# The last MoE batch written out, with dummy products on TensorE ahead of the last expert's down units and its scatter

## The reference, cut to what matters

```python
def expert_choice_moe(h, w_router, w1, w3, w2):      # N_EXPERTS = 16, EXPERT_FF = 1024
    cap = EC_CAPACITY * S // N_EXPERTS               # 32 tokens for each expert
    aff = jax.nn.softmax(jnp.einsum('bsd,de->bse', h, w_router), axis=-1)
    vals, idx = lax.top_k(aff.transpose(0, 2, 1), cap)
    xg = h[bidx, idx]
    h1 = jnp.einsum('becd,edf->becf', xg, w1)
    h3 = jnp.einsum('becd,edf->becf', xg, w3)
    out = jnp.einsum('becf,efd->becd', jax.nn.silu(h1) * h3, w2) * vals[..., None]
    return jnp.zeros_like(h).at[bidx, idx].add(out)
...
x = x + expert_choice_moe(rmsnorm_2(x, norm_moe[i]), ...)
ple_gate = jax.nn.sigmoid(rmsnorm_2(x, norm_ple[i]) @ ple_gate_w[i])
x = x + ple_gate * (p[i] @ ple_w[i])
```

## Time and profile before

| | us |
|---|---|
| median of 3 runs | 1885.49 |
| lowest, highest | 1884.97, 1887.38 |
| span of the profiled execution, first to last instruction | 1886.9 |
| TensorE busy | 1546.9 (82%) |
| chain that ended last, waits for `moe_w` transfers | 37% |

### The profile page before, as it was taken

How to read it: one execution, slowest core, us unless ns; L and a number is a source line. 1 busy time by engine, 2 the same in 40 slices (tenths; PEclk the granted TensorE clock), 3 DMA queues, 4 the chain that set the end, 5 groups by cost and what they waited for, 6 DMA issues and landing times.

```text
span 1886.9 us, 29888 instructions
## 1 busy us (share of the span) xinstructions
PE 1546.9 (82%) x12670; PEld 1134.2 (60%) x12670; DVE 633.5 (34%) x934; ACT 517.6 (27%) x921; POOL 193.9 (10%) x215
## 2 busy tenths in 40 slices
PE   9999999999999999656665666999998665666657
PEld 8999899998798885232322324997873322223225
DVE  3556653677656452000000003655540000000005
ACT  3434344556444532000000003454521000000003
POOL 1042000011141100000000002310100000000003
PEclk9999999999999999898888878999999888988888
DMA  9364679423554479999999999644499999999994
GB/s 305 122 211 164 210 234 290 135 90 113 182 166 140 136 318 380 424 426 425 424 428 426 427 425 348 197 146 149 174 381 405 423 427 423 429 425 426 427 424 144
DMA packets 166895, 563.67 MB, mean 299 GB/s; under 512 B 10559, under 2 KB 120027, under 8 KB 133896
## 3 DMA queue, kind: packets, MB, share of 16 engines
q1 hardware_dynamic: 161092, 553.88, 76.0%
q10 hardware_dynamic: 5700, 8.31, 1.3%
HBM read 561.08 MB, written 5.23 MB: 300 GB/s over the span
## 4 chain that ended last, share of the span: by engine, by line
PE 51%; DMA 37%; DVE 4%; issue 3%; ACT 3%; POOL 1%; ACTq 0%; DVEq 0%; POOLq 0%; SPq 0%
DMA ring<-in_moe_w 37%; PE bank L1003 20%; PE bank L1271 7%; PE bank L1685 4%; PE bank L955 3%; PE bank L1334 2%; PE bank L1708 2%; PE bank L1118 1%; ACT ring_r L1758 1%; PE bank L1110 1%; PE bank L1148 1%; PE bank L1543 1%; ACT big L1806 1%; PE bank L1343 1%; PE bank L1083 1%
## 5 line engine op out<-in xcount | busy, mean ns | idle before, releaser
L1685 PE MATMUL bank<-ring,big 128*32 128x256 f32 x3840 | 281.6, 443 | 196.2 <-DMA ring<-in_moe_w 193.8
L1003 PE MATMUL bank<-big_r,ring_r 128*128 128x256 f32 (+1 forms) x2856 | 355.4, 284 | 0.0
L1685 PEld LDWEIGHTS bank<-ring,big 128*32 128x32 f32 x3840 | 146.4, 123 | 337.9 <-issue 296.7
L1003 PEld LDWEIGHTS bank<-big_r,ring_r 128*128 128x128 f32 (+1 forms) x2856 | 346.2, 191 | 3.0 <-issue 2.2
L2156 DVE TENSOR_TENSOR ring_r<-ring,ring_r 128x2048 fp32r<-128x2048 f32 (+2 forms) x113 | 260.1, 2307 | 135.9 <-ACT ring_r L1758 134.6
L1806 ACT ACTIVATE big<-bank 128x512 f32<-128x512 f32 (+2 forms) x186 | 87.9, 491 | 561.8 <-PE bank L955 355.6
L1758 ACT ACTIVATE ring_r<-ring 128x2048 fp32r<-128x2048 f32 (+2 forms) x117 | 219.3, 1884 | 13.2 <-issue 7.3
L1708 PE MATMUL bank<-ring,big 128*32 128x512 f32 x1024 | 137.5, 634 | 74.8 <-DMA ring<-in_moe_w 57.7
L2551 DVE SCALAR_TENSOR_TENSOR big<-big,bank 128x256 f32<-128x256 f32 x32 | 13.5, 421 | 460.1 <-ACT big L2059 460.1
L1271 PE MATMUL bank<-ring_r,big_r 128*128 128x512 f32 x576 | 136.6, 396 | 0.7 <-DVE big_r L2163 0.7
L1271 PEld LDWEIGHTS bank<-ring_r,big_r 128*128 128x128 f32 x576 | 107.9, 189 | 25.5 <-DVE ring_r L2156 1.1
(11 more groups left out here) (213 smaller groups left out, 1474.5 us busy)
## 6 DMA issues: line engine op xcount, KB each, us to landing
ring<-in_moe_w SPq DMA_DIRECT2D x120, 2048.0 KB, 23.7
ring<-in_moe_w SPq DMA_DIRECT2D x128, 1024.0 KB, 24.9
ring<-in_w_in SPq DMA_DIRECT2D x28, 1024.0 KB, 5.4
ring<-in_od_w_in SPq DMA_DIRECT2D x22, 1024.0 KB, 6.0
ring<-in_ev_w_in SPq DMA_DIRECT2D x20, 1024.0 KB, 5.5
big<-in_moe_w SPq DMA_DIRECT2D x8, 2048.0 KB, 11.0
ring<-in_ev_w_out SPq DMA_DIRECT2D x8, 1024.0 KB, 5.0
ring<-in_od_cmp_w SPq DMA_DIRECT2D x8, 1024.0 KB, 8.3
```

Of the source, the lines that this page charges most:

```text
L1003: ins = unit[0].mark(mm(dst, lhsT, rhs, start=start and n == 0, stop=stop and n == len(terms) - 1))
L1685: ins = mm(banks[5 + up][32 * j:32 * j + 32, 0:256], xg[:, k, q, :], wv[:, r, 256 * j:256 * (j + 1)], start=k == 0, stop=k == KC - 1)
```

## The change

The last batch is taken out of the hardware loop, which now makes two trips, and is written out behind it. Conditions that asked whether a batch is written out now ask for batch 0. In the last expert of the last batch (`closing`), TensorE runs three dummy products ahead of each of the four down units, before it waits for the unit, and one dummy product between the last down unit and the wait for `ob_ready` ahead of the scatter. A dummy multiplies the identity (128x128) with 256 columns of constants into columns 256 to 511 of bank 6, which nothing reads. That makes 13 dummies for each of the two layers. Nothing else differs, on no other engine.

```diff
+                def keep_warm(n):
+
+                    for _ in range(n):
+                        mm(banks[6][:, T:2 * T], ident, big[:, con_at:con_at + T], start=True, stop=True)
+
...
-                                spare = isinstance(b, int) and q < 2 and part == 1
+                                spare = isinstance(b, int) and b == 0 and q < 2 and part == 1
...
-                        if isinstance(b, int) and q == 0:
+                        if isinstance(b, int) and b == q == 0:
                             keep_after(3)
...
                         pe.wait_ge(hT_ready, m + 1)
+                        closing = isinstance(b, int) and b > 0 and q == BATCH - 1
                         for j in range(4):
+                            if closing:
+                                keep_warm(3)
                             U = Unit()
...
                         ins.then_inc(down_done, 1)
+                        if closing:
+                            keep_warm(1)
                         pe.wait_ge(ob_ready, m + 1)
...
                 batch(0)
-                with pe.Fori(0, NE // BATCH - 1) as b:
+                with pe.Fori(0, NE // BATCH - 2) as b:
                     w.enter(b, BATCH * MOE_UNITS)
                     batch(b + 1)
-                    w.leave(NE // BATCH - 1)
+                    w.leave(NE // BATCH - 2)
+                batch(NE // BATCH - 1)
```

## The result

The change takes 1893.0 us in the median of 5 runs (1891.88 to 1894.64) against 1885.49 (1884.97 to 1887.38) before: a ratio of 1.0039, 95% interval 1.0029 to 1.0050. Run again beside 27 runs of the kernel before, it gave 1893.87 against 1886.16, ratio 1.0038 (1.0024 to 1.0051). So it is 7 to 8 us slower. I had forecast 0.6.

What follows compares the result with a forecast made beforehand. In the MoE stages TensorE waits for weights from a full DMA. Dummies delay the fourth down unit more than the held clock gains: 14.10 against 13.79 and 13.78, 0.3 a layer, 0.6 in sum, 1886.1 us; range 1884.0 to 1888.8.

Steps and rivals of the forecast that it cites:

- my 0.3: Forecast delay of DVE's split, line 2115, in each layer: 14.10 against 13.79 and 13.78 us after the first down unit's start.
- Call it zero: Last expert: times counted from the first down unit's start, 1153.00 and 1838.97; everything up to it hides under `moe_w` transfers.
- The base, line 2115 at 13.79 and 13.78: Before the change, DVE's split was taken to start 13.79 and 13.78 us after the first down unit, first and second layer.
- 1.4 under that span: The runs' median, 1885.49, stands 1.4 us under the profiled span, 1886.9; the same 0.6 was added to both.
- 0.1 for each change: Each change of form between dummies and down units costs 0.1 us; seven ahead of the fourth unit, 0.7.
- my 8.44: Fourth down unit's start after the first group began: dummies 5.16, three down units 2.58, seven changes of form 0.7.
- my 3.85: From the scatter's start, forecast at 10.25, to DVE's split at 14.10, at full clock with four DVE copies.
- 14.10: Forecast start of DVE's split, line 2115, after the change, in us from the start of the last expert's dummies.
- the way back: Change from full-width products to column groups, read between the gather and the first up unit as 0.08 us.
- rival (b): Each change of form drains the array, 0.36 us each: 2.1 later a layer, 4.3 in sum, 1889.8 us; chance 0.04.
- which continuous products should hold: From the fourth down unit on, full clock: unit 1.06, scatter 1.99; gains 0.88 and 1.6, only partly reaching the chain.
- Rival (c): Clock falls despite the dummies, before the last group, or had fallen when they begin: 3.4 later a layer, 1892.3 us; chance 0.03.

Runs made afterwards that it cites:

- before_again: The kernel before, unchanged, run again for a second profile: 1886.53 us, ratio 0.9998.
- written_out_only: The change with no dummies at all, only the last batch written out: 1889.3 us, ratio 1.0010 against the kernel before.
- gaps_only: The change with three dummies ahead of only the third and fourth down units, one ahead of the scatter: 1886.67 us, ratio 0.9998 against the kernel before.
- first_two_groups: The change with three dummies ahead of only the first and second down units, one ahead of the scatter: 1885.49 us, ratio 0.9996 against the kernel before.
- in_the_loop: Kernel before, batch not written out; each looped batch's last expert gets three dummies before down units three and four, one before the scatter: 1885.68 us, ratio 0.9996.
- in_the_loop_and_behind: in_the_loop plus one dummy between scatter and tile 0's transposes and two before the first gate products: 1885.22 us, ratio 1.0003 against the kernel before.
- two_each: The change with two dummies instead of three ahead of each down unit, one ahead of the scatter: 1888.62 us, ratio 1.0013 against the kernel before.
- three_without_last: The change without dummies ahead of the fourth down unit, three ahead of the others, one ahead of the scatter: 1888.86 us, ratio 1.0017 against the kernel before.
- change_and_up_parts: The change plus three dummies ahead of each of the last expert's four up parts: 1891.44 us, ratio 1.0034 against the kernel before.
- change_again: The change, unmodified, run again for a second profile: 1893.87 us, ratio 1.0038 against the kernel before.
- change_and_behind: The change plus one dummy between scatter and tile 0's transposes and two before the first gate products: 1893.32 us, ratio 1.0037 against the kernel before.
- six_dummies: The change with six dummies instead of three ahead of each down unit, one ahead of the scatter: 1902.97 us, ratio 1.0088 against the kernel before.

## Why the prediction was wrong

**The direction and the mechanism were right.** Four groups make TensorE late at the fourth unit, the wait on the DMA goes, and the clock holds. The place is shown by the number of dummies: level with before with two groups (either two), +2.9 with two dummies each, +3.1 with three groups, +7.7 with all, +16.0 with twice as many (medians, each against the kernel before of its own set). The size was off by more than ten times: the sum began in the wrong place, and it stood on an unusual execution. The account, from the start of the fourth up part to DVE's split (timelines, us, first and second layer):

| kernel | fourth up part takes | to line 2115 or its like |
|---|---|---|
| before | 1.93, 1.93 | 17.58, 17.57 |
| before_again | 1.93, 1.93 | 16.62, 16.54 |
| written_out_only | 1.93, 1.93 | 17.64, 16.69 |
| gaps_only | 3.30, 1.93 | 16.50, 15.46 |
| first_two_groups | 3.51, 3.35 | 16.57, 16.35 |
| in_the_loop | 3.33, 3.64 | 16.51, 18.97 |
| in_the_loop_and_behind | 1.93, 1.93 | 15.56, 15.42 |
| two_each | 1.93, 1.93 | 16.47, 16.47 |
| three_without_last | 1.93, 1.93 | 16.57, 16.57 |
| change_and_up_parts | 1.93, 1.93 | 18.19, 18.19 |
| change | 1.93, 3.64 | 18.20, 20.16 |
| change_again | 1.93, 3.64 | 18.20, 21.99 |
| change_and_behind | 2.78, 3.64 | 20.85, 21.99 |
| six_dummies | 3.39, 3.41 | 25.01, 24.85 |

The kernel before has 17.1 in the mean of its two profiles; change, change_again and change_and_behind have 20.2: 3.1 a layer, 6.3 in all, of 7.7 measured. Of the 2.8 a layer above my 0.3, the slow parts make 2.0 (20.2 against 18.20), the base 0.5, the changes of form 0.35.

**1. "Call it zero": the first down unit's start.** This step failed, and by the table it is the largest part. I took the start of the first down unit as the same before and after, because all ahead of it "hides under `moe_w` transfers". It does not come at a fixed time after the landing: the fourth up part takes 1.93, or up to 3.64 when it meets the low clock. The kernel before hides this. Its own trace shows it, one expert ahead of the last in the first layer:

```profile
1119.71 3.64 PE L1685 MATMUL bank<-ring,big 128*32 128x256 f32 x32 [1.28 <-DMA ring<-in_moe_w]
...
1125.47 2.78 PE L1708 MATMUL bank<-ring,big 128*32 128x512 f32 x24 [0.52 <-issue]
...
1149.21 1.93 PE L1685 MATMUL bank<-ring,big 128*32 128x256 f32 x32 [1.46 <-DMA ring<-in_moe_w]
```

The fourth unit still waits 1.28 for its transfer, and the scatter starts at 1131.35, 11.64 after the part; in the last expert, with a part of 1.93 at 1149.21, it is 12.67. The two profiles of the kernel before have 28 experts each whose fourth part and down units wait for transfers. In 33 of these 56 the fourth part is slow (2.77 to 3.64). In 28 of the 33 the scatter starts 11.64 to 11.67 after the part's start and takes 1.99. In the 23 with a part of 1.93 it starts 11.61 to 12.67 after it, and takes 3.29 to 3.68 in all but one. So before the change a slow part mostly costs nothing, and even leaves the clock up for the scatter.

With the wait on the DMA gone, so is the cover: the delay goes through in full, and where the first dummies meet the low clock as well, more than in full (18.20 to 21.99). I had counted what the dummies cost, but not what the removed wait had absorbed. Four of the six ends of change, change_again and change_and_behind have a slow part. It does not need all four groups: in_the_loop's second layer, with two, comes at 18.97. In time it is shown less well: 1.9 us between change_and_behind and change_and_up_parts, with overlapping intervals.

**2. The base, line 2115 at 13.79 and 13.78.** The rows were right, but of an execution with the low clock in the last down unit of both layers. before_again has 12.82 and 12.74: by it the base was 1.0 too late in each layer. A run's time lies 1.8 over its span (1886.53 for 1884.7, 1893.78 for 1892.0), so the profiled execution of before was a run of about 1888.7, above all that I had timed. I had read the median "1.4 under that span" as an offset, when it said that the profiled execution took longer than the timed ones. And both profiles may flatter the change: their four ends all have a fast fourth part and then a slow scatter. For an end with a slow part, 11.65 to the scatter and 3.68 from a full-clock scatter to the split (as in every end with one here) would make 15.3, an estimate. No profile caught such an end of the kernel before.

**3. "0.1 for each change".** The fourth unit starts at 8.96 against my 8.44. A dummy is 0.43 as predicted (3.78 - 2.49 = 1.29 for three more), so the seven changes cost 8.96 - 5.16 - 2.58 = 1.22, 0.17 each, within my bounds of 0 and 0.36. The fourth unit is 0.52 later than forecast; from the scatter to line 2126 it then takes 3.68 for my 3.85, so 0.35 is left there (14.45 for 14.10). The sum behind the 0.1 was loose as well: it names 0.118 a record and computes with 0.115, and with 0.118 the way back would have cost nothing. The Trainium skill's rule, "TensorEngine Tiling (Array Packing)", Key Properties, that changing the mode drains the array, bears more than I gave it; rival (b) in its full size, 0.36, did not come.

**4. The clock "which continuous products should hold".** It held through the scatter. Rival (c) named 1892.3, close to what was measured, but for another reason: a fall ahead of the last group, which no profile has. Its other condition, a clock that "had fallen when they begin", did come, in the second layers of change_again and change_and_behind: the first group takes 2.93 for 1.56 there. In the change's first profile the clock then fell 5 us after the scatter began, behind the stretch with 1.09 busy of 2.80, on the first gate products: 1.43 in each layer, and in neither of the second profile, though the same stretch has 1.09 busy there too. In the kernel before's two profiles the low clock lay on the scatter and had risen again by line 1334. So part of what the dummies buy at one place may be paid at the next. A slow line 1334 does reach the end of the program: from the second layer's split (line 2115 or its like) to the end of the span it is 35.56 to 35.60 in the three profiles that have one there (change, three_without_last, change_and_up_parts), and 34.10 to 34.44 in the other eleven. That filling the stretch keeps line 1334 at full clock fits two profiles, but is not shown: the profiles beside them had the full clock without it.

**5. The forecast that the batch written out is worth nothing** stands within some 2 us: 1.0010 in the kernel that has nothing else, 0.9998 and 0.9996 in two that have dummies too. The instruction queue carried 0.19 MB more (1.47 for 1.28), where I had estimated 0.12 for both layers. Whether its 12 packets cost anything stays open.

What also stays open: the rest of about 1.4 us between 6.3 and 7.7, and why two_each and three_without_last are 2.9 and 3.1 slower than before, though their profiles (16.47, 16.57) are level with before_again. Two terms could fill it, and neither is shown to: the gate products (2.9 in one of three profiles, 1 in the mean), and ends of the kernel before with a slow part. If these are as frequent as in its other experts, 33 of 56, its mean end is 16.1 and not 17.1, by the estimate of 15.3. A few profiles can't give a distribution.

No version tried is measurably faster than the kernel before.

## What to carry to other kernels

Filler in a wait is free only as long as the sum of filler and work stays under the arrival of the last transfer, and it also uses up the slack that absorbs a late start, even where it stands only ahead of units that really wait. Check the sum against the last landing with every preceding stage at its slower duration; the slower durations can be found in the same stage of other iterations, in the profile that you have. Before a stretch is priced from one profile, compare that execution's own time with the runs: if it lies above them, its slow stretches are not the usual ones. And a clock kept high at one place can be lost again at the next wait.

## What the runs showed of the hardware

- The same up part of the same kernel takes 1.93 or up to 3.64 us from one execution to the next (at 1060.66 in one profile of the kernel before, at 1059.97 in the other). The scatter takes 1.99 to 3.77. The kernel before spreads over 1883.0 to 1889.7 us in its runs here, 0.4%.
- In the kernel before, the two go against each other: behind a slow fourth part the scatter ran at full clock in 30 of 33 experts, behind a fast one in 1 of 23.
- A change between full-width products and column groups and back costs about 0.34 us in this stream, 0.17 each on average, over the products' own 0.43 and 0.86.
- The low clock can come behind a stretch of 2.80 us with 1.09 busy, 5 us after the start of a scatter at full speed, and the same stretch can also leave the clock up.
